# Five places for x, gate products with the narrow weight held in the array, and the samples' page attention with the pages as the moving operand

## The chip, the cores and the metric

The kernel runs on one core of one Trainium2 chip. The metric is the device time of one execution in microseconds, as a median over runs. The profiled execution is one more run of the same program; its trace is what the rows below are from.

## What is computed

One step of a decoder layer with two kinds of token: 528 prompt tokens (16 learned ones and 512 of the prompt) and 32 sample tokens (8 sequences of 4 new tokens, each with 256 cached tokens in two pages of 128). Cut to what matters here:

```python
xn = rmsnorm(h, norm_mix)                          # 560 rows of 2048
p  = xn @ w_in                                     # q, k, v, z, og of 8 + 8 heads, and three narrow parts:
a, b, f = p[..., C_A:C_Z] (2 x 8 columns), p[..., C_F:C_OG] (8 columns)
g, beta, logf = gates of a, b, f                   # per token and head
# attention of the samples, per head; c is the running sum of logf over page 0, page 1 and the new tokens
s = q @ k_past.T * scale + c_q - c_k               # 4 new tokens of a sequence against its own 256 cached ones
o = softmax([s, s_new]) @ [v_past, v_new]
```

Behind it come the gated delta rule of the other eight heads, the output product and a retrieval of experts for every token.

## The kernel before

One program runs its stages one behind the other, with a barrier of all engines between them: `norm_and_gates` (all 560 tokens, in tiles of 128, 128, 128, 128 and 48), then for the FIRST group of tokens (256: the 32 samples and 224 of the prompt) `heads`, `mix_out`, `ffn_norm` and `route`, then the same for the LATER group (304 tokens) with the gathering of experts beside it, then `rest_of_experts`. The traces name the tiles of the two `heads` stages `heads_a_...` and `heads_b_...`; the samples are in `heads_a` alone.

**norm_and_gates.** Rows of x come into two places (`lead.rows`), so tile i can be loaded when tile i - 2 has been turned. ScalarE squares and sums a tile (L432) and takes the root (L435), VectorE makes the reciprocal (L468) and scales the tile (L470), TensorE turns it in 16 blocks (L528), VectorE moves these out in four pieces, with the gain (L475), to `xnT`, the turned tokens. The 24 narrow columns (a, b, f) are made at the end: for each tile 16 products with `xnT` as the operand that is held in the array and the 24 columns of `w_narrow` streamed past it (L536). VectorE copies the result (L483) and the gates and running sums follow. Ahead of its first tile VectorE waits for the page table and makes row numbers of it (L458 to L463), from which GpSimd gathers cached values (L415).

**heads.** Each engine follows an order written down as marks in numbers: `Marks` runs several generators (the delta rule, the fox attention, the projections), each of which yields the mark of its next step, and the lowest mark goes first. TensorE's projections (L879, 16 products of 256 columns for each of 64 segments) lie between the other steps. `sampled` is TensorE's part for the samples' attention: it turns 16 pages of keys (L1051), makes the scores of the cached tokens with the pages held in the array and the 4 queries of a sequence as the moving operand (L1069, 16 products; L1063, L1066 and L1067 add the running sums), turns the scores (L1080), and after the exponential makes the output with 16 products that hold a page of values and move 4 columns (L1094). ScalarE and VectorE copy between these steps (L1586, L1592, L1593, L1326).

A product of 32-bit numbers stands in the trace as two instructions of TensorE (records, below), a transpose as one. In a row, `128*32` is partitions and columns of what is held in the array, and `128x128` what is streamed.

Of the kernel before, what the change touches and what calls it, by code (L numbers as in the profile page):

```python
# [22 lines left out]
ALU = mybir.AluOpType  # L23
# [6 lines left out]
P = 128  # L30
D = 2048
# [72 lines left out]
def constant_parts():  # L104
# [24 lines left out]
        "causal0": np.where(same0 & (col <= row) | (row >= NS), 0.0, NEG)[:, :NS],  # L129
        "batch_cols": np.broadcast_to((np.arange(NS)[None, :] // NQ == np.arange(NB)[:, None]).reshape(1, -1),  # L130
# [196 lines left out]
def norm_and_gates(nc, ins, outs, mem, scr, group):  # L327
# [4 lines left out]
        "const_in first_in vec_rows_in narrow_in bias_in pages_in x_in0 x_in1 x_squared x_root x_scaled x_turned "  # L332
# [6 lines left out]
            "cT": ([HEADS, 2, group.cols],),  # L339
# [3 lines left out]
        {"turn": [P, 4, 512], "nar": [P, T, 32], "cps": [HEADS, 2 * BANK], "vps": [P, P]},  # L343
# [12 lines left out]
    loaded = [16 * sum(len(parts[j]) for j in range(i % 2, i + 1, 2) if j >= early) for i in range(T)]  # L356
    with ctx:
        x, sq, ss, rt, rs = lead.rows, buf["sq"], buf["ss"], buf["rt"], buf["rs"]
# [7 lines left out]
        def _(sp):  # L366
            if samples:
                for rows, source in parts[0]:
                    sp.dma_start(x[rows, 0, :], source).then_inc(sem["x_in0"], 16)
# [51 lines left out]
        def _(act):  # L421
            if samples:
                act.wait_ge(sem["const_in"], 16)
            for i in range(T):
                r = group.rows[i]
                if i < early:
                    act.wait_ge(lead.landed[i], ready[i])
                else:
                    act.wait_ge(sem[f"x_in{i % 2}"], loaded[i])
                if i >= 1:  # L430
                    act.wait_ge(sem["x_squared"], i)
                nc.scalar.activation(sq[0:r, :], x[0:r, i % 2, :], ACT.Square, accum_out=ss[0:r, i:i + 1]  # L432
                                     ).then_inc(sem["x_squared"], 1)
# [2290 lines left out]
```

## Time and profile before

| | |
|---|---|
| median of 3 runs | 4275.11 us (4270.05 to 4278.51) |
| the profiled execution, its own time | 4273.7 us |
| its span, first to last instruction | 4271.9 us |
| granted TensorE clock, mean | 0.864 of 2.4 GHz |
| norm_and_gates | 0 to about 94 us |
| heads_a | about 94 to 936 us |

A row of the timeline gives the start from the span's start, the duration, the engine, the line and what it did, with xcount where several of one kind follow each other; behind it stands how long the engine was idle ahead and who ended that. A row of windows gives the busy time of each engine in a stretch with the number of instructions in brackets, then the granted clock (PEclk; 1.00 is 2.4 GHz, 0.50 is 1.2 GHz), the DMA engines' share and their rate.

### The profile page before, as it was taken

To read this page: it belongs to the slowest core of one execution; us is meant where nothing else is said; L and a number is where in the kernel's file an instruction comes from. 1 tells how busy PE (TensorE), PEld (TensorE's weight loads), DVE (VectorE), ACT (ScalarE), POOL (GpSimd) and SP (SyncE) were. 2 spreads that over 40 slices of the span, in tenths; PEclk is the share of its full clock that TensorE was granted. 3 is DMA by queue.
4 is the path that set the end of the run, shared out by engine and by line. 5 is a ranking of instruction groups with operands and counts; after the bars stand their busy time and mean duration, and the time that the engine had idled before them with its cause. 6 is when DMAs were issued, how large, how long until landed. Compare 5 with 4: busy or idle time off the path is not lost. (4 is left out here: it accounts for less than half of the span.)

```text
span 4271.9 us, 40765 instructions
## 1 busy us (share of the span) xinstructions
PE 3365.5 (79%) x14471; PEld 2616.6 (61%) x14471; DVE 2772.4 (65%) x4327; ACT 683.8 (16%) x1807; POOL 1587.5 (37%) x1091
## 2 busy tenths in 40 slices
PE   5999999989979999998949784000237999999994
PEld 5888888878856667666637563000136766666663
DVE  2233333320679999998986788699899655555655
ACT  1222222310112222223210011000124000000000
POOL 1000110100245555553563444588763322223222
PEclk7999999979989999999959897555555999999997
DMA  3766666648879999999999972899998999999997
GB/s 88 238 207 207 203 204 205 200 148 290 259 304 407 397 394 389 389 393 371 390 381 391 386 269 93 350 422 422 383 379 298 383 421 422 421 422 422 422 421 286
DMA packets 435530, 1396.72 MB, mean 327 GB/s; under 512 B 37188, under 2 KB 283608, under 8 KB 285264
## 3 DMA queue, kind: packets, MB, share of 16 engines
q0 software_dynamic: 125040, 890.66, 52.1%
q1 hardware_dynamic: 297616, 402.79, 27.3%
q10 hardware_dynamic: 12672, 100.67, 6.0%
q8 instruction: 115, 1.88, 0.2%
q14 instruction: 87, 0.71, 0.0%
HBM read 1258.98 MB, written 134.87 MB: 326 GB/s over the span
## 5 line engine op out<-in xcount | busy, mean ns | idle before, releaser
L1948 DVE CUSTOM_DVE_ANT_0 ex_ring<-ex_ring,ex_xi 128x2048 f32<-128x2048 f32 x544 | 1240.1, 2288 | 295.0 <-DMA ex_ring<-in_peer_u_dram,idx_all 205.3
L1899 POOL DMA_INDIRECT ex_ring<-in_peer_u_dram,idx_all x384 | 620.0, 1614 | 580.0 <-DVE ex_hid L1948 507.5
L1961 DVE SCALAR_TENSOR_TENSOR ex_y<-ex_ring,ex_wt,ex_y 128x2048 f32<-128x2048 f32 x285 | 677.9, 2379 | 233.3 <-DMA ex_ring<-in_peer_v_dram,idx_all 223.5
L879 PE MATMUL heads_b_pj<-xnT_later,lead 128*128 128x304 f32 x2048 | 595.6, 428 | 26.9 <-PEq L289 20.6
L1899 POOL DMA_INDIRECT ex_ring<-in_peer_v_dram,idx_all x256 | 397.4, 1552 | 571.9 <-DVE ex_y L1961 501.9
L2642 PE MATMUL rest_acc<-lead,rest_wide_act 128*128 128x512 f32 x1024 | 450.6, 598 | 6.6 <-DMA lead<-in_peer_v_dram 5.7
L879 PEld LDWEIGHTS heads_b_pj<-xnT_later,lead 128*128 128x128 f32 x2048 | 371.6, 194 | 134.5 <-issue 27.3
L2642 PE MATMUL rest_acc<-xnT_later,rest_wide_act 128*128 128x512 f32 x1024 | 444.7, 592 | 0.0
L2642 PEld LDWEIGHTS rest_acc<-lead,rest_wide_act 128*128 128x128 f32 x1024 | 304.2, 297 | 147.9 <-DMA lead<-in_peer_v_dram 7.1
L2642 PEld LDWEIGHTS rest_acc<-xnT_later,rest_wide_act 128*128 128x128 f32 x1024 | 302.1, 295 | 137.3
L1899 POOL DMA_INDIRECT ex_ring<-in_peer_u_dram,ex_idx_s x160 | 296.5, 1853 | 209.1 <-DVE ex_hid L1948 163.1
L2614 PE MATMUL rest_acc<-const,S_kept 128*128 128x128 f32 x4 | 1.4, 448 | 432.2 <-DVE S_kept L2667 432.2
L879 PE MATMUL heads_a_pj<-xnT_first,heads_a_w 128*128 128x256 f32 x1216 | 316.4, 398 | 2.4 <-DMA heads_a_w<-in_w_in_dram 2.4
L2614 PEld LDWEIGHTS rest_acc<-const,S_kept 128*128 128x128 f32 x4 | 0.6, 203 | 432.9 <-DVE S_kept L2667 432.9
L879 PEld LDWEIGHTS heads_a_pj<-xnT_first,heads_a_w 128*128 128x128 f32 x1216 | 226.7, 199 | 33.0 <-issue 2.9
L879 PE MATMUL heads_a_pj<-xnT_first,lead 128*128 128x256 f32 x832 | 213.7, 396 | 4.9 <-PEq L289 4.9
L1920 ACT ACTIVATE ex_act<-ex_hid 128x16 f32<-128x16 f32 x34 | 7.4, 216 | 1310.9 <-DVE ex_hid L1948 1310.9
L879 PEld LDWEIGHTS heads_a_pj<-xnT_first,lead 128*128 128x128 f32 x832 | 155.6, 199 | 25.6 <-issue 7.0
L2625 PE MATMUL rest_acc<-rest_hot_col,rest_hot_row 128*128 128x128 f32 x256 | 66.4, 441 | 103.4 <-DVE rest_hot_col L2692 103.4
L2054 PE MATMUL out_b_acc<-out_b_w,mixT_b 128*128 128x256 f32 (+1 forms) x672 | 147.4, 380 | 0.0
L2054 PEld LDWEIGHTS out_b_acc<-out_b_w,mixT_b 128*128 128x128 f32 (+1 forms) x672 | 111.5, 168 | 35.8 <-issue 4.7
L2625 PEld LDWEIGHTS rest_acc<-rest_hot_col,rest_hot_row 128*128 128x128 f32 x256 | 57.0, 328 | 112.9 <-DVE rest_hot_col L2692 112.9
(594 smaller groups left out, 4621.7 us busy)
## 6 DMA issues: line engine op xcount, KB each, us to landing
lead<-w_scratch SPq DMA_DIRECT2D x64, 1024.0 KB, 9.2
lead<-in_peer_v_dram SPq DMA_DIRECT2D x64, 1024.0 KB, 9.1
xnT_later<-in_peer_v_dram SPq DMA_DIRECT2D x64, 1024.0 KB, 9.0
heads_a_w<-in_w_in_dram SPq DMA_DIRECT2D x38, 1024.0 KB, 6.1
w_scratch<-heads_a_w ACTq DMA_DIRECT2D x38, 1024.0 KB, 4.6
lead<-in_w_in_dram SPq DMA_DIRECT2D x26, 1024.0 KB, 6.2
w_scratch<-lead ACTq DMA_DIRECT2D x26, 1024.0 KB, 4.4
out_a_w<-in_w_out_dram SPq DMA_DIRECT2D x7, 2048.0 KB, 14.0
```

What stands on the lines that cost most here:

```text
L879: last = nc.tensor.matmul(pj[j % PJ][:, 0:N], slot(j)[:, k, :], xnT[:, k, :], start=(k == 0), stop=(k == KT - 1))
L1899: pool.indirect_dma_start(self.ring[:, i % RING, :], None, self.tables[which], bass.IndirectOffsetOnAxis(ap=self.index(s, g, k), axis=0)). ...
L1920: self.nc.scalar.activation(self.act[:, g % 2, :], self.hid[:, g % 2, :], ACT.Gelu).then_inc(self.sem["activated"], 1)
L1948: nc.vector.tensor_tensor_reduce(ring, ring, self.tokens(s)[:], 1.0, 0.0, ALU.mult, ALU.add, self.hid[:, g % 2, k:k + 1]).then_inc(self.se ...
L1961: nc.vector.scalar_tensor_tensor(y, ring, wt, y, ALU.mult, ALU.add).then_inc(self.sem["consumed"], 1)
L2054: last = nc.tensor.matmul(acc[0:b - a, i, 0:GW], mixT[:, k, a:b], weights[:, k, :], start=(k == 0), stop=(k == KT - 1))
L2614: last = nc.tensor.transpose(acc[:, d, i * P:(i + 1) * P], source, cst("ident"))
L2625: last = nc.tensor.matmul(out, hot_row[:, n % 2, j, :], hot_col[:, n % 2, j, :], start=True, stop=True)
L2642: last = nc.tensor.matmul(acc[:, d, b:b + BANK], weights(d, quarter, c), v_place(n)[:, b:b + BANK], start=(n == 0), stop=(n == KEYS - 1))
```

## The change

It has two parts. In `norm_and_gates`: five places for x, so that SyncE issues all loads without waiting; ScalarE waits for the constants after its first square and no longer ahead of it; the row numbers of the pages are made after tile 1; the 24 narrow columns are made "flat", with `w_narrow` (24 columns) held in the array and 256 or 304 tokens streamed past it, those of FIRST after tile 3 and those of LATER at the end, then copied by ScalarE and turned back by five transposes. In `sampled`: queries and probabilities are spread over the eight sequences with zeros elsewhere (`q_apart`, `P_apart`), 32 columns each, and held in the array; the pages are streamed, 256 columns (both pages of a sequence) for the scores and 128 for the output. The results of four sequences lie in four groups of 32 output partitions, and two products with a constant (`strips`) add the four groups up.

```diff
@@ norm_and_gates, SyncE
-                if i >= 2:
-                    sp.wait_ge(sem["x_turned"], 4 * (i - 1))
-                for rows, source in parts[i] if i >= max(early, 1) else []:
-                    sp.dma_start(x[rows, i % 2, :], source).then_inc(sem[f"x_in{i % 2}"], 16)
+                for rows, source in parts[i] if i >= 1 else []:
+                    sp.dma_start(x[i][rows, :], source).then_inc(sem[f"x_in{i}"], 16)
...
-            for s in sorted(range(2), key=lambda s: T - 1 - (T - 1 - s) % 2):
-                sp.wait_ge(sem["x_turned"], 4 * (T - (T - 1 - s) % 2))
+            for s in range(2):
+                sp.wait_ge(sem["x_turned"], 4 * (s + 1))
@@ ScalarE
-            if samples:
-                act.wait_ge(sem["const_in"], 16)
...
+                if i == 0:
+                    act.wait_ge(sem["const_in"], 16)
                 act.wait_ge(sem["x_squared"], i + 1)
...
+            for n, (at, of) in enumerate(((0, FIRST), (BANK, LATER))):
+                act.wait_ge(sem["flat_done"], n + 1)
+                nc.scalar.copy(buf["flat"][:, of.base:of.base + of.cols], cps[:, at:at + of.cols]).then_inc(sem["flat_copied"], 1)
@@ VectorE
+                if i == 1:
+                    page_rows()
@@ TensorE
+                if i == 3 or i == T - 1:
+                    of, turned, at = (FIRST, mem["xnT"], 0) if i == 3 else (LATER, mem["xnT_later"], BANK)
+                    pe.wait_ge(sem["narrow_in"], 32)
+                    pe.wait_ge(sem["x_evac"], 4 * FIRST.n if i == 3 else 4 * T)
+                    for k in range(KT):
+                        last = nc.tensor.matmul(cps[:, at:at + of.cols], buf["w_narrow"][:, k, :], turned[:, k, :],
+                                                start=(k == 0), stop=(k == KT - 1))
+                    last.then_inc(sem["flat_done"], 1)
+            pe.wait_ge(sem["flat_copied"], 2)
             for i, (a, b) in enumerate(group.tiles):
-                for k in range(KT):
-                    last = nc.tensor.matmul(nar[0:b - a, i, 0:24], turned_place(k, i), buf["w_narrow"][:, k, :],
-                                            start=(k == 0), stop=(k == KT - 1))
+                last = nc.tensor.transpose(nar[0:b - a, i, 0:24], buf["flat"][:, a:b], cst("ident")[0:24, 0:24])
@@ heads, TensorE, sampled
-                for page in (1, 0):
-                    out = B.F1[:, page * NS:(page + 1) * NS].rearrange("p (b q) -> p b q", b=NB)
-                    nc.tensor.matmul(out, cst("after", P, 2 * P), past[:, :, page:page + 1].to_broadcast([P, NB, NQ]),
-                                     start=True, stop=False)
-                    if page == 0:
-                        nc.tensor.matmul(out, ones, later, start=False, stop=False)
-                    nc.tensor.matmul(B.F1[:, page * NS:(page + 1) * NS], ones, B.lU[:, 0:NS], start=False, stop=False)
-                    for b in range(NB):
-                        last = nc.tensor.matmul(B.F1[:, page * NS + NQ * b:page * NS + NQ * (b + 1)], B.kc[:, 2 * b + page, :],
-                                                q0[:, NQ * b:NQ * (b + 1)], start=False, stop=(b == NB - 1))
+                pe.wait_ge(sem["q_apart"], n)
+                for b in range(NB):
+                    strip = slice(b % 4 * NS, (b % 4 + 1) * NS)
+                    last = nc.tensor.matmul(B.F1[strip, 0:2 * P], B.q_apart[:, b, :],
+                                            B.kc[:, 2 * b:2 * b + 2, :].rearrange("p n c -> p (n c)"), start=(b < 4), stop=(b >= 4))
...
-                    last = nc.tensor.transpose(B.F2[0:NS, page * P:(page + 1) * P], B.sT[:, page * NS:(page + 1) * NS], ident)
+                    out, late = B.F2[0:NS, page * P:(page + 1) * P], B.lU[:, 0:NS] if page else B.late_q[:]
+                    nc.tensor.matmul(out, B.past_q[:, page, :], cst("after", P, 2 * P), start=True, stop=False)
+                    nc.tensor.matmul(out, late, ones, start=False, stop=False)
+                    last = nc.tensor.matmul(out, cst("strips"), B.sS[:, page * P:(page + 1) * P], start=False, stop=True)
...
-                nc.tensor.matmul(sums, B.f_vN[0:NS, 0, :], B.sPT[0:NS, 2 * NS:], start=True, stop=False)
-                for b in range(NB):
-                    for page in range(2):
-                        last = nc.tensor.matmul(sums[:, NQ * b:NQ * (b + 1)], B.vc[:, 2 * b + page, :],
-                                                B.sPT[:, page * NS + NQ * b:page * NS + NQ * (b + 1)],
-                                                start=False, stop=(b == NB - 1 and page == 1))
+                nc.tensor.matmul(sums[0:NS, :], B.sPT[:], B.f_vN[0:NS, 0, :], start=True, stop=False)
+                for i in range(4):
+                    for strip in range(4):
+                        b, page = 4 * (i // 2) + strip, i % 2
+                        last = nc.tensor.matmul(sums[strip * NS:(strip + 1) * NS, :], B.P_apart[:, b, page, :], B.vc[:, 2 * b + page, :],
+                                                start=(i == 0 and strip > 0), stop=(i == 3))
...
-                nc.tensor.transpose(B.F2[0:NS, 0:HD], B.sO[:], ident).then_inc(sem["s_rows"], 1)
+                nc.tensor.matmul(B.F2[0:NS, 0:HD], cst("strips"), B.sO[:], start=True, stop=True).then_inc(sem["s_rows"], 1)
@@ heads, VectorE
+                        order.mark(nc.vector.tensor_copy(B.past_q[:].rearrange("p n (b q) -> p n b q", b=NB), past))
+                        nc.vector.tensor_tensor(B.late_q[:], B.past_q[:, 1, :], B.lU[:, 0:NS], ALU.add
+                        nc.vector.tensor_tensor(B.q_apart[:], qkv[:, 0, 0:NS].unsqueeze(1).to_broadcast([P, NB, NS]),
...
-                        nc.vector.tensor_copy(B.sT[:], B.F1[:, 0:2 * NS]).then_inc(sem["scores_copied"], 1)
+                        nc.vector.tensor_copy(B.sS[:], B.F1[:, 0:2 * P]).then_inc(sem["scores_copied"], 1)
...
-                        order.mark(nc.vector.tensor_copy(B.sPT[:, 0:2 * NS], B.F1[:, 0:2 * NS]))
+                        order.mark(nc.vector.tensor_tensor(
+                            B.P_apart[:], B.F1[:, 0:2 * NS].rearrange("p (n q) -> p n q", n=2).unsqueeze(1).to_broadcast(shape),
```

The marks are as they were. TensorE's order in the second fox head, from before the scores to the turned scores, was this (the last number of a row is what comes out, L879 the projections, L970 the delta rule):

```order
L879 MATMUL heads_a_pj<-xnT_first,lead 128x256 x2
L1063 MATMUL heads_a_F<-heads_a_lpast,const 128x32
L1067 MATMUL heads_a_F<-heads_a_lU,const 128x32
L1069 MATMUL heads_a_F<-heads_a_f_qkvT,heads_a_kc 128x4 x8
L1063 MATMUL heads_a_F<-heads_a_lpast,const 128x32
L1066 MATMUL heads_a_F<-heads_a_lpast,const 128x32
L1067 MATMUL heads_a_F<-heads_a_lU,const 128x32
L1069 MATMUL heads_a_F<-heads_a_f_qkvT,heads_a_kc 128x4 x8
L1074 MATMUL heads_a_F<-heads_a_f_qkvT 32x32
L1075 MATMUL heads_a_F<-const,heads_a_lU 32x32
L1076 MATMUL heads_a_F<-const_first,const 32x32
L879 MATMUL heads_a_pj<-xnT_first,lead 128x256 x4
L970 MATMUL heads_a_R<-heads_a_yX,heads_a_EN 128x128 x2
L879 MATMUL heads_a_pj<-xnT_first,lead 128x256
L1080 MATMUL heads_a_F<-const,heads_a_sT 32x128 x2
```

The same place of the changed kernel (its L889 and L980 are the projections and the delta rule):

```order
L889 MATMUL heads_a_pj<-xnT_first,lead 128x256 x2
L1072 MATMUL heads_a_F<-heads_a_kc,heads_a_q_apart 32x256 x8
L1077 MATMUL heads_a_F<-heads_a_f_qkvT 32x32
L1078 MATMUL heads_a_F<-const,heads_a_lU 32x32
L1079 MATMUL heads_a_F<-const_first,const 32x32
L889 MATMUL heads_a_pj<-xnT_first,lead 128x256 x4
L980 MATMUL heads_a_R<-heads_a_yX,heads_a_EN 128x128 x2
L889 MATMUL heads_a_pj<-xnT_first,lead 128x256
L1084 MATMUL heads_a_F<-const,heads_a_past_q 32x128
L1085 MATMUL heads_a_F<-const,heads_a_late_q 32x128
L1086 MATMUL heads_a_F<-heads_a_sS,const_first 32x128
```

21 products stood ahead of L1074 and now 8; where two transposes stood, six products stand (the second three, for the other page, read `lU` in place of `late_q`). Nothing else moved on TensorE here; at the output 16 products of 4 columns became 16 of 128 columns in four groups of 32 partitions, in the same place.

On TensorE in `norm_and_gates` the changed kernel has this order, where all of tile 4's transposes used to come ahead of the 80 products of 24 columns:

```order
L532 MATMUL norm_a_turn<-const,norm_a_x_more 128x128 x32
L541 MATMUL norm_a_cps<-xnT_first,norm_a_w_narrow 24x256 x16
L532 MATMUL norm_a_turn<-const,norm_a_x_more 128x48 x16
L541 MATMUL norm_a_cps<-xnT_later,norm_a_w_narrow 24x304 x16
L546 MATMUL norm_a_nar<-const,norm_a_flat 128x24 x4
L546 MATMUL norm_a_nar<-const,norm_a_flat 48x24
```

32 products stand where 80 stood, and half of them ahead of the last tile's transposes.

## Rows read from the trace of the kernel before

**Rows 1.** The page: busy time and share of TensorE.
```profile
PE 3365.5 (79%) x14471; PEld 2616.6 (61%) x14471; DVE 2772.4 (65%) x4327; ACT 683.8 (16%) x1807; POOL 1587.5 (37%) x1091
```
**Rows 2.** Windows: heads_a with projections, and its last 49 us.
```profile
122.00:887.00 765.00, 748.07 (x4263) 652.01 (x4264) 253.05 (x746) 207.64 (x497) 76.13 (x86) 0.95 0.67 203
887.00:936.00 49.00, 38.77 (x188) 30.78 (x186) 11.92 (x31) 8.85 (x26) 2.85 (x2) 0.64 0.22 75
```
**Rows 3.** Timeline of norm_and_gates: start, us, engine, line, what, idle before.
```profile
10.83 1.91 ACT L432 ACTIVATE norm_a_sq<-lead 128x2048 f32<-128x2048 f32 x1 [1.65 <-DMA const<-in_constants_dram]
14.14 0.29 ACT L435 ACTIVATE norm_a_rt<-norm_a_ss,const 128x1 f32<-128x1 f32 x1
16.48 0.43 SPq L391 DMA_DIRECT2D pages<-in_page_table_dram  x1
20.28 0.17 DVE L458 CAST norm_a_rowf<-pages 128x16 f32<-128x16 int32 x1 [7.12 <-DMA pages<-in_page_table_dram]
20.84 0.16 DVE L468 RECIPROCAL norm_a_rs<-norm_a_rt 128x1 f32<-128x1 f32 x1
26.08 12.79 SPq L384 DMA_DIRECT2D lead<-in_x_prompt_dram  x3
26.70 0.15 DVE L468 RECIPROCAL norm_a_rs<-norm_a_rt 128x1 f32<-128x1 f32 x1
30.93 1.91 ACT L432 ACTIVATE norm_a_sq<-lead 128x2048 f32<-128x2048 f32 x1 [14.25 <-DMA lead<-in_x_prompt_dram]
79.72 0.53 DVE L483 COPY norm_a_narrow<-norm_a_nar 128x24 f32<-128x24 f32 x5 [30.35 <-PE norm_a_nar L536]
```
**Rows 4.** Timeline of TensorE in norm_and_gates: the last turned tile, the narrow products.
```profile
47.07 1.91 PE L528 MATMUL norm_a_turn<-const,lead 48*128 48x48 f32 x16 [2.95 <-DVE lead L470]
63.17 16.51 PE L536 MATMUL norm_a_nar<-norm_a_w_narrow,xnT_later 128*128 128x24 f32 x96
```
**Rows 5.** Windows of norm_and_gates: clock through the narrow products, and behind.
```profile
47.20:88.00 40.80, 35.41 (x193) 33.90 (x194) 3.65 (x18) 2.05 (x5) 0.00 (x0) 0.50 0.18 44
88.20:94.90 6.70, 1.83 (x16) 1.34 (x15) 2.04 (x11) 0.00 (x0) 0.00 (x0) 1.00 0.04 5
```
**Rows 6.** Timeline of the second fox head: a page copy, then the scores.
```profile
275.78 0.69 DVE L1582 COPY heads_a_kc<-heads_a_F 128x512 f32<-128x512 f32 x1 [1.41 <-PE heads_a_F L1051]
282.02 0.30 PE L1063 MATMUL heads_a_F<-heads_a_lpast,const 128*128 128x32 f32 x2
282.38 1.93 PE L1069 MATMUL heads_a_F<-heads_a_f_qkvT,heads_a_kc 128*128 128x4 f32 x16
284.17 0.39 PE L1063 MATMUL heads_a_F<-heads_a_lpast,const 128*128 128x32 f32 x2
287.21 0.32 PE L1074 MATMUL heads_a_F<-heads_a_f_qkvT 128*32 128x32 f32 x2
```
**Rows 7.** Timeline of TensorE: products with 32 held columns, and the output.
```profile
397.88 1.93 PE L994 MATMUL heads_a_R<-heads_a_state,heads_a_apart 128*32 128x128 f32 x16
399.75 1.99 PE L879 MATMUL heads_a_pj<-xnT_first,lead 128*128 128x256 f32 x8
402.23 4.00 PE L1094 MATMUL heads_a_F<-heads_a_sPT,heads_a_vc 128*128 128x4 f32 x32
```
**Rows 8.** Windows: through the scores, behind them, and behind the output.
```profile
282.70:286.00 3.30, 3.30 (x32) 3.30 (x31) 0.00 (x0) 0.00 (x0) 0.00 (x0) 1.00 0.97 236
286.10:292.80 6.70, 6.70 (x26) 5.69 (x27) 0.65 (x2) 0.00 (x0) 0.00 (x0) 0.50 0.12 33
405.60:408.90 3.30, 3.30 (x11) 2.76 (x11) 0.00 (x0) 0.19 (x1) 0.00 (x0) 0.50 0.47 114
```
**Rows 9.** Timeline of TensorE: 32 held columns, and two halves of the array's rows.
```profile
909.71 3.62 PE L1013 MATMUL heads_a_R<-heads_a_state,heads_a_apart 128*32 128x128 f32 x16
...
3241.80 11.16 PE L2631 MATMUL rest_acc<-rest_hot_col,rest_hot_row 64*128 64x128 f32 x64 [0.83 <-issue]
```
**Rows 10.** Window over the 64 records of the last row of rows 9.
```profile
3242.10:3253.00 10.90, 10.83 (x64) 10.27 (x62) 9.75 (x23) 6.08 (x25) 1.86 (x2) 0.50 0.84 283
```

More of the change, by code:

```diff
@@ L129, in constant_parts @@
         "causal0": np.where(same0 & (col <= row) | (row >= NS), 0.0, NEG)[:, :NS],
+        "strips": row % NS == np.arange(NS)[None, :],
         "batch_cols": np.broadcast_to((np.arange(NS)[None, :] // NQ == np.arange(NB)[:, None]).reshape(1, -1),
@@ L338, in norm_and_gates @@
             "bias": ([P, 3, HEADS],), "af": ([P, T, 16],), "ab": ([P, T, 16],), "ea": ([P, HEADS],),
-            "cT": ([HEADS, 2, group.cols],),
+            "cT": ([HEADS, 2, group.cols],), "x_more": ([P, T - 2, D],), "flat": ([24, group.cols],),
             **({"vec_rows": ([V_END, P],), "rowf": ([P, PAGES],), "rowi": ([P, PAGES], I32)}
@@ L355, in norm_and_gates @@
     ready = list(lead.counts)
-    loaded = [16 * sum(len(parts[j]) for j in range(i % 2, i + 1, 2) if j >= early) for i in range(T)]
+    assert early == 0
     with ctx:
-        x, sq, ss, rt, rs = lead.rows, buf["sq"], buf["ss"], buf["rt"], buf["rs"]
+        x = [lead.rows[:, i, :] if i < 2 else buf["x_more"][:, i - 2, :] for i in range(T)]
+        sq, ss, rt, rs = buf["sq"], buf["ss"], buf["rt"], buf["rs"]
         turn, nar, cps, vps = buf["turn"], buf["nar"], buf["cps"], buf["vps"]
@@ L368, in _ @@
                 for rows, source in parts[0]:
-                    sp.dma_start(x[rows, 0, :], source).then_inc(sem["x_in0"], 16)
+                    sp.dma_start(x[0][rows, :], source).then_inc(sem["x_in0"], 16)
                 lasting = mem["const"].shape[1]
@@ L421, in _ @@
         def _(act):
-            if samples:
-                act.wait_ge(sem["const_in"], 16)
             for i in range(T):
                 r = group.rows[i]
[L426 to L429, printed above, removed]
+                act.wait_ge(sem[f"x_in{i}"], 16 * len(parts[i]))
                 if i >= 1:
                     act.wait_ge(sem["x_squared"], i)
-                nc.scalar.activation(sq[0:r, :], x[0:r, i % 2, :], ACT.Square, accum_out=ss[0:r, i:i + 1]
+                nc.scalar.activation(sq[0:r, :], x[i][0:r, :], ACT.Square, accum_out=ss[0:r, i:i + 1]
                                      ).then_inc(sem["x_squared"], 1)
+                if i == 0:
+                    act.wait_ge(sem["const_in"], 16)
                 act.wait_ge(sem["x_squared"], i + 1)
@@ L455, in _, with page_rows @@
                                         0.5, None, ALU.mult).then_inc(sem["vecs_ready"], 1)
+            def page_rows():
                 dve.wait_ge(sem["pages_in"], 16)
@@ L541, in _ @@
             for i in range(T):
-                out, s = cps[:, i * P:(i + 1) * P], group.slot + i
+                out, s = cps[0:HEADS, i * P:(i + 1) * P], group.slot + i
                 block_of = min(s, 1)
@@ L648, in heads @@
                 "kc": ([P, PAGES, HD],), "vc": ([P, PAGES, HD],),
-                "sT": ([P, 2 * NS],), "sP": ([NS, KS],), "sPT": ([P, 3 * NS],),
-                "sO": ([P, NS],), "sN": ([NS, HD],), "smax": ([NS, 1],), "sden": ([NS, 1],), "srec": ([NS, 1],)}
+                "sS": ([P, 2 * P],), "sP": ([NS, KS],), "sPT": ([NS, NS],), "q_apart": ([P, NB, NS],),
+                "P_apart": ([P, NB, 2, NS],), "past_q": ([P, 2, NS],), "late_q": ([P, NS],),
+                "sO": ([P, HD],), "sN": ([NS, HD],), "smax": ([NS, 1],), "sden": ([NS, 1],), "srec": ([NS, 1],)}
                if samples else {"kT_kept": ([P, KA],), "v_kept": ([P, FIRST.n, HD],)}),
@@ L1325, in fox @@
                         act.wait_ge(sem["s_out"], n)
-                        nc.scalar.copy(B.sO[:], B.F1[:, 2 * P:2 * P + NS]).then_inc(sem["s_outT"], 1)
+                        nc.scalar.copy(B.sO[:], B.F1[:, 2 * P:2 * P + HD]).then_inc(sem["s_outT"], 1)
                     for i in range(1, T + 1):
```

31 lines of the change are left out of this document (17 added, 14 removed).

## The prediction

> **What bounds the kernel now.** The page comes first: TensorE is busy for 79% of the span [rows 1], and the stages run one behind the other, so what a stage loses or wins stays in the end time unless a later one gives it back. The next view is the windows by stage. From 122 to 887 us, heads_a with its projections, TensorE is busy for 748 of 765 us, VectorE for 253 and the DMA engines for 0.67 of it [rows 2]: TensorE is the bound there, and what is taken from it comes off the end. Its granted clock is 0.95 on the mean. The last 49 us of the stage have no projections left between the steps and a clock of 0.64 [rows 2].
>
> The timeline of norm_and_gates shows three things. VectorE stands idle for 7.1 us until the page table has landed, makes row numbers at 20.28 and starts tile 0 at 20.84, although ScalarE had its root at 14.43 [rows 3]. The third x tile is issued at 26.08, when its place is free, and ScalarE has it at 30.93 [rows 3]. From the end of the last turned tile, 48.98, to 79.72 nothing runs but 80 products of 24 columns [rows 3, 4], at 1.2 GHz [rows 5].
>
> **First stage, step by step.** ScalarE's first square loses its 1.65 us wait for the constants, so the root is there at 14.43 - 1.65 = 12.8 [rows 3]. VectorE has its gain vectors by then (they are what it did ahead of its 7.12 us of idling, 20.28 - 7.12 = 13.16). Tile 0 starts at 13.2 where it was 20.84: 7.6 us. A tile takes VectorE 26.70 - 20.84 = 5.86 us. The third x tile is issued behind the page table's row, 16.48 + 0.43 = 16.9, and needs 30.93 - 26.08 = 4.85 us [rows 3] and 2.4 of ScalarE (1.91, 0.29 and the reading of the sum): 24.2, where VectorE ends tile 1 at 13.2 + 2 x 5.86 = 24.9. So no load is waited for, and with 0.56 us for the row numbers (20.28 to 20.84) VectorE is through tile 3 at 37.2, TensorE's transposes 0.7 earlier.
>
> Then the flat products of FIRST: 16 of 256 columns. For their price I take a group of 32 held and 128 streamed columns, 16 records from 397.88 to 399.75, 0.117 us each, or 0.47 us for a product of 256 columns; at 1.2 GHz 16 such records took 3.62, 0.226 each, or 0.90 [rows 7, 9]. Sixteen cost 7.5 to 14.5 us; I take 9.5, since a stretch of streamed products with 8 held columns came ahead of the rise at 88.2 [rows 5]. Tile 4's transposes and last copy come to 2.4 (1.91 [rows 4] and half a us), and LATER's 16 products of 304 columns to 8.9 at 2.4 GHz (17.2 at 1.2). ScalarE's copy and five transposes I put at 1.5, an estimate from the 0.69 of a copy of 512 columns [rows 6] and 0.12 per record. Sum: 36.5 + 9.5 + 2.4 + 8.9 + 1.5 = 58.8 against 79.72: 21 us. All at 1.2 GHz gives 36.5 + 14.5 + 2.4 + 17.2 + 1.5 = 72.1, a gain of 8; all at 2.4 GHz, with shorter transposes, 54, a gain of 26. I take **-21**. The row numbers are made at 25 us instead of 20, and GpSimd's gather hides behind the flat products. Weights for heads_a are now loaded into places that come free after tiles 0 and 1, behind all x tiles in SyncE's queue.
>
> **Samples' attention, step by step, at 2.4 GHz.** Products that hold a page cost 16 records in 284.17 - 282.38 = 1.79 us, 0.112 each, whatever little they stream [rows 6]. Before, a head has 21 for the scores, 17 for the output and three transposes: 79 records, 8.8 us. After, if every product waits for the one ahead: scores 16 records of 256 columns, 32 x 0.112 = 3.6; the two sets of three products, 12 records with a change of shape in them at 0.117, 1.4; output 34 records, 3.8; the last product 0.3. That is 9.1, or **+0.3** a head, +3 us in all: as a plain rewrite it gives nothing. It pays if the four groups of 32 columns run at once. At best the scores cost 0.9 and the output 0.95 + 0.2, in all 3.8, **-5.0** a head.
>
> No row shows column groups side by side. The nearest is products on two halves of the array's rows: 64 records took 11.16 us at 1.2 GHz [rows 9, 10], 0.174 each with waits, where one group of columns took 0.226. The two halves do run beside each other, though in that order eight of one half stand ahead of eight of the other. The new order changes group after every product. I take most of the best, -4.3 a head, **-34** in all, and keep +3 and -40.
>
> A rule speaks against this. The Trainium skill, "TensorE: Matmul & The Clock Gate", Part 3, says that a load of weights overlaps products in flight only when they are on other rows of the array; the four groups share all rows. By it every load would be exposed. In the trace sixteen records on the same rows and the same columns took 0.117 each, with no room for an exposed load [rows 7]. The same part gives 2.4 times for three column groups, and by that figure the scores and output would cost about 2.7 us, an estimate between my two ends.
>
> **The clock.** While the scores run, TensorE is busy for all of the time with 4-column products at 2.4 GHz; right behind, 6.7 us are at 1.2 GHz, and after the output another 3.3 [rows 8]. In this time projections take twice as long. The windows put a size on it: (1 - 0.95) x 765 = 38 us lost at full rate in 765 us [rows 2]. Some 4 of it I leave to other places. After the change no long run of 4-column products is left; the group of 16 records with 32 held and 128 streamed columns has no fall behind it: 8 records of projections follow in 1.99 us, 0.25 each for 256 columns, the rate of 2.4 GHz [rows 7]. I take **-30**: all of the 34 but a little, and a few of the last 49 us. If the falls stay it is 0.
>
> **What is added elsewhere.** VectorE gets two small copies, `q_apart` (256 columns), a copy of 256 instead of 64 columns and `P_apart` (512 columns, 0.69 by the page copy [rows 6]): about 2 us a head, on an engine busy for a third of the time [rows 2]. Behind `q_apart` waits a delta-rule sum, behind `P_apart` the output; in both places TensorE has projections and delta-rule products ahead of the step that reads them. If both were exposed it would be 1.1 us a head, 9 in all. ScalarE's wider copy is hidden likewise. In the last head nothing covers them, 1 us. I add +1.
>
> **Sum.** 4273.7 (the profiled execution) - 21 - 34 - 30 + 1 = 4189.7. The median of the runs is 1.4 above that execution: **4191 us**.
>
> **Rivals.**
> - *The groups don't overlap.* For: no row shows it, and the rule above. Against: the halves of rows. 4191 + 37 = 4228.
> - *Overlap, but the clock still falls* as often: TensorE stands in shorter pieces then, and in the stage's last part, made of short pieces, it has 0.64 [rows 2]. 4191 + 30 = 4221. Neither: 4258.
> - *A new wait takes the place.* The output is short now, and behind it TensorE comes sooner to the sum that waits for VectorE's masked copy of u, begun with the output; scores come sooner after the page copies. If half of the 34 + 30 goes: 4223.
> - *The first stage gains little*, with x late or all at 1.2 GHz: 4204, within the first case's range.
> - *Slower.* One mechanism: the granted clock in heads_a stays at 1.2 GHz for long after each of the new groups. Every us at 1.2 costs half a us of streaming. With the other gains in place (85), it must be 170 us more, 21 us of each head's 102 (765 us hold seven and a half heads), before the kernel is slower. The old falls last 10 us a head, and the groups with 32 held columns caused none.
> - *No change* within 0.2% (8.6 us, what a measurement of this kernel can tell): the parts would have to cancel each other.
>
> **How the numbers follow.** Overlap and a steady clock 0.52, own range 4170 to 4212; no overlap 0.22; overlap with falls 0.08; a new wait 0.08; neither 0.05; no change 0.02; slower 0.03. The range reaches over the first four: 4170 to 4236. Faster 0.95, same 0.02, slower 0.03.
>
> **What would show it.** In the changed trace: VectorE's reciprocal of tile 0 at 13 us; the copy of the narrow results at 56 to 62 and heads_a's first projection near 74; PEclk of the windows through heads_a at 0.98 or more; eight products of the scores in about 1 us (overlap) or 3.5 (none), and heads 93 us apart instead of 102. It is wrong if the sampled products keep 0.2 us per 256-column record from start to start, if falls of the clock still follow them, or if TensorE shows idle time ahead of L1019's product or of the scores.

## The result and the profile after

The changed kernel takes 4166.9 us (median of 4 runs, 4166.22 to 4169.49) against 4276.81 of before (4 runs, 4270.05 to 4281.82): ratio 0.9748, 95% interval 0.9732 to 0.9763. The forecast was 4191 us, 4170 to 4236: the direction was right, and the time lies 3 us below the range. The same two kernels, measured once more among the experiments on the first stage, gave 4169.24 and 4271.89: a gain of 103 us where it is 110 here. The profiled execution took 4166.22 us, its span 4164.3, at a mean clock of 0.877.

The first stage, in the timeline of the changed kernel (ScalarE's third square, TensorE, and VectorE's copy of the narrow results; it answers to [rows 3, 4]):

```profile
23.73 1.91 ACT L427 ACTIVATE norm_a_sq<-norm_a_x_more 128x2048 f32<-128x2048 f32 x1 [6.95 <-DMA norm_a_x_more<-in_x_prompt_dram]
...
35.44 7.09 PE L541 MATMUL norm_a_cps<-xnT_first,norm_a_w_narrow 128*24 128x256 f32 x32
42.45 1.19 PE L532 MATMUL norm_a_turn<-const,norm_a_x_more 48*128 48x48 f32 x16
46.01 9.73 PE L541 MATMUL norm_a_cps<-xnT_later,norm_a_w_narrow 128*24 128x304 f32 x32 [2.36 <-issue]
...
56.72 0.53 DVE L487 COPY norm_a_narrow<-norm_a_nar 128x24 f32<-128x24 f32 x5 [10.86 <-PE norm_a_nar L546]
```

The narrow results are copied at 56.72 us where it was 79.72 [rows 3]. The flat products of FIRST took 7.09 us. Ahead of LATER's TensorE stands idle for 2.36 us, waiting for VectorE's four pieces of tile 4. The program asks for this wait, but VectorE stood idle for 0.50 and 1.08 us ahead of the last two pieces, which started at 44.06 and 45.50, while TensorE was through with the tile at 43.64; where none is late, in the trace of the first part alone, the idle time is 0.59 us. This comes up again in the last experiments.

The samples' attention in the third fox head (timeline of TensorE; it answers to [rows 6, 7]):

```profile
340.65 1.07 PE L1072 MATMUL heads_a_F<-heads_a_kc,heads_a_q_apart 128*32 128x256 f32 x16
341.54 0.22 PE L1077 MATMUL heads_a_F<-heads_a_f_qkvT 128*32 128x32 f32 x2
...
341.82 1.99 PE L889 MATMUL heads_a_pj<-xnT_first,heads_a_w 128*128 128x256 f32 x8
...
354.95 1.08 PE L1101 MATMUL heads_a_F<-heads_a_vc,heads_a_P_apart 128*32 128x128 f32 x32
355.96 0.92 PE L889 MATMUL heads_a_pj<-xnT_first,lead 128*128 128x256 f32 x3
```

The start of the next row tells what a group cost: 16 records of the scores, each of 256 columns, are through in 341.54 - 340.65 = 0.89 us, and the 32 of the output in 355.96 - 354.95 = 1.01. The projections right behind the scores run at 8 records in 1.83 us (341.82 to 343.65), which is the rate of 2.4 GHz, where [rows 8] had 1.2. The windows of before show the same from afar; here are those of the changed kernel:

```profile
103.60:816.70 713.10, 695.62 (x4287) 592.15 (x4285) 262.11 (x767) 209.60 (x502) 78.55 (x87) 1.00 0.71 220
816.80:834.70 17.90, 7.54 (x27) 4.49 (x27) 5.19 (x15) 7.32 (x20) 0.96 (x1) 0.69 0.10 30
```

For 713 us the clock does not fall once (0.95 in [rows 2]), and the fall to 1.2 GHz in the tail begins with 18 us left, not with 46. No wait of any size took the place of the old work (waits of TensorE in heads_a, changed kernel: us in total, times, longest):

```profile
PE heads_a_R L1045 <- DVE heads_a_gU L1550: 8.7, 8, 1.8
PE heads_a_R L953 <- DVE heads_a_qkvT L1472: 8.1, 8, 1.0
```

Before the change these two waits had the same 8.7 and 8.1 us. The only new one is 0.5 us, once, for ScalarE's exponential. From the first product of one stage to that of the next, in us:

| | before | changed | difference | forecast |
|---|---|---|---|---|
| norm_and_gates | 94.6 | 72.0 | -22.6 | -21 |
| heads_a | 841.9 | 762.8 | -79.1 | -63 |
| everything behind | 3335.4 | 3329.6 | -5.8 | 0 |

### The profile page after: what moved, and what is told of

It is laid out like the page before. It is cut to its first block and busy times, and to the rows that moved or that the text cites. A ratio compares the mean times of both kernels' runs of the same rounds, so it can differ in the third digit from the quotient of the medians.

```text
span 4164.3 us, 40395 instructions
## 1 busy us (share of the span) xinstructions
PE 3266.1 (78%) x14260; PEld 2508.1 (60%) x14260; DVE 2779.5 (67%) x4351; ACT 685.4 (16%) x1809; POOL 1607.5 (39%) x1091
## 5 line engine op out<-in xcount | busy, mean ns | idle before, releaser
L1916 POOL DMA_INDIRECT ex_ring<-in_peer_u_dram,idx_all x384 | 633.3, 1649 | 572.4 <-DVE ex_hid L1965 498.8
L889 PE MATMUL heads_b_pj<-xnT_later,lead 128*128 128x304 f32 x2048 | 594.2, 428 | 26.1 <-PEq L290 21.4
L889 PEld LDWEIGHTS heads_b_pj<-xnT_later,lead 128*128 128x128 f32 x2048 | 371.3, 194 | 133.9 <-issue 28.3
L889 PE MATMUL heads_a_pj<-xnT_first,heads_a_w 128*128 128x256 f32 x1216 | 302.5, 384 | 2.2 <-DMA heads_a_w<-in_w_in_dram 2.2
L889 PEld LDWEIGHTS heads_a_pj<-xnT_first,heads_a_w 128*128 128x128 f32 x1216 | 217.1, 191 | 31.3 <-issue 5.7
L889 PE MATMUL heads_a_pj<-xnT_first,lead 128*128 128x256 f32 x832 | 206.3, 385 | 4.9 <-PEq L290 4.9
L889 PEld LDWEIGHTS heads_a_pj<-xnT_first,lead 128*128 128x128 f32 x832 | 150.4, 192 | 24.8 <-issue 8.4
## 6 DMA issues: line engine op xcount, KB each, us to landing
out_a_w<-in_w_out_dram SPq DMA_DIRECT2D x7, 2048.0 KB, 14.7
```

The costliest lines, as they stand in the source:

```text
L889: last = nc.tensor.matmul(pj[j % PJ][:, 0:N], slot(j)[:, k, :], xnT[:, k, :], start=(k == 0), stop=(k == KT - 1))
L1916: pool.indirect_dma_start(self.ring[:, i % RING, :], None, self.tables[which], bass.IndirectOffsetOnAxis(ap=self.index(s, g, k), axis=0)). ...
```

## The experiments

**Each part alone.** One kernel with the edits inside `norm_and_gates`, one with all others; both are the diff shown above, cut in two.

> The kernel before with the first part alone (norm_and_gates). In the changed kernel heads_a begins 22.6 us earlier. Theory 1 (each part gives its gain in its own stage): 22 to 24 us less than before, 4252 to 4255, with the clock falls of heads_a as before. Rival (the earlier loads of the first weights or the earlier start shift something in heads_a, and this is where the surplus over the prediction comes from): 28 us or more less, with heads_a itself more than 4 us shorter than its 838.7.

> The kernel before with the second part alone (the samples' attention). Theory 1 (four column groups run wholly at once, 4.9 us a head at 2.4 GHz, and no fall of the clock is left, 4.2 us a head and some 12 us in the last 49 us of the stage): 80 to 88 us less than before, 4189 to 4197, PEclk 1.00 through heads_a. Rival (part of the surplus hangs on both parts together): under 76 us less.

Measured: first part alone 4238.61 us (4235.74 to 4243.11), 0.9917 of before (0.9901 to 0.9934), 34 less; second part alone 4193.74 (4190.93 to 4197.94), 0.9812 (0.9796 to 0.9829), 79 less. The second lies within the expected 4189 to 4197, though its gain is 1 us short of the expected 80 to 88. The first does not lie within its 4252 to 4255: of its 34 us its trace shows 22.3 in the stage itself, 3.3 in heads_a and 5.4 behind it, so the 28 or more of the rival came true in the sum but not by its reason: heads_a was not over 4 us shorter. The 3.3 are in the clock (table of heads_a below). The parts add up to 113 where both together gave 110, and 103 when measured again, within what the runs scatter.

**Column groups.** The changed kernel with all products of the scores and the output in the first 32 output partitions:

```diff
-                    last = nc.tensor.matmul(B.F1[strip, 0:2 * P], B.q_apart[:, b, :],
-                                            ..., start=(b < 4), stop=(b >= 4))
+                    last = nc.tensor.matmul(B.F1[0:NS, 0:2 * P], B.q_apart[:, b, :],
+                                            ..., start=(b == 0), stop=(b == NB - 1))
...
-                        last = nc.tensor.matmul(sums[strip * NS:(strip + 1) * NS, :], ...
+                        last = nc.tensor.matmul(sums[0:NS, :], ...
```

> The changed kernel with all sampled products in one group of 32 columns (output partitions 0 to 31; the other 96 rows of sS and sO are set to zero once), so that the same 24 products of a head follow each other. Theory 1 (overlap is worth 2.6 us at the scores and 2.6 at the output of each head, and the clock does not depend on it): 42 us over the changed kernel, 4207 to 4211, PEclk still 1.00. Rival (the dense use of four groups is what keeps the clock up): 70 us over it, 4237, with falls to 1.2 GHz behind the scores. Second rival (the page's rule: loads of weights on the same rows are exposed, 24 products more than streaming): over 0.115 us a record of 128 columns and 55 us or more over it.

Measured: 4202.57 us (4200.57 to 4208.13), 0.9833 (0.9817 to 0.985), 36 more than the changed kernel, heads 97.8 us apart where they were 92.6. Its windows and lines, the records of seven heads:

```profile
122.00:800.00 678.00, 664.06 (x3839) 561.44 (x3838) 236.65 (x697) 185.37 (x447) 67.92 (x76) 1.00 0.69 215
```
```profile
L1100 PE MATMUL heads_a_F<-heads_a_vc,heads_a_P_apart 128*32 128x128 f32 x224 | 25.8, 273 | 0.0
...
L1071 PE MATMUL heads_a_F<-heads_a_kc,heads_a_q_apart 128*32 128x256 f32 x112 | 25.5, 381 | 0.0
```

The same 16 records of the scores are busy for 25.5 / 7 = 3.64 us, where the rows of the changed kernel have 1.07, and the 32 of the output for 3.69 instead of 1.08. From the first start to that of the next work, as above, it is 3.48 instead of 0.89 and 3.61 instead of 1.01. So the groups overlap, and by almost all of the factor of four that is there: 3.9 and 3.6. The median is 4 us below the expected 4207 to 4211; heads_a is 42.9 us longer than in the changed kernel, where the expectation had 42. The clock stays at 2.4 GHz: it does not need the overlap.

**The clock alone.** The kernel before with its 4-column products unchanged in number and form, but put in pairs between the projections. Only marks differ:

```diff
                     for b in range(NB):
+                        if b % 2 == 0:
+                            yield at + 17 + 3.5 * (1 - page) + 0.85 * (b // 2)
...
+                    yield at + 31.5 + 0.7 * b
```

> The kernel before with its products of 4 columns unchanged in number and kind, but given out two at a time between projections (the marks of the sampled steps behind them are moved by 1 to 5). Theory 1 (what makes the clock fall is that 32 such products follow each other): the falls of heads_a with projections vanish, 4.2 us a head, 25 to 40 us less than before, 4236 to 4251. Rival A (the falls come with the number of such products, however they lie): within 8 us of before. Rival B (waits brought by the moved marks eat it): PEclk up to 0.99 but TensorE idle over 2 us a head.

Measured: 4240.3 us (4235.86 to 4244.58), 0.9924 (0.9907 to 0.994), 32 less than before with exactly the old work, and within the 4236 to 4251 of Theory 1. Its windows, and two rows of its timeline:

```profile
122.00:800.00 678.00, 662.72 (x3965) 580.13 (x3963) 228.02 (x667) 188.40 (x452) 68.53 (x76) 1.00 0.72 218
```
```profile
277.06 0.68 PE L879 MATMUL heads_a_pj<-xnT_first,lead 128*128 128x256 f32 x2
277.57 0.51 PE L1071 MATMUL heads_a_F<-heads_a_f_qkvT,heads_a_kc 128*128 128x4 f32 x4
```

The falls behind the scores and outputs are gone (1.00 for 0.95), and all that was gained is theirs: what made the clock fall was that 32 records of 4 columns followed each other without a pause, not their number. The last 49 us of the stage kept their low clock (33.8 us at 1.2 GHz for 36.0).

**Which run brings which fall.** The changed kernel with the scores new and the output in its old form (the lines of the output and its copies as in the removed half of the diff above):

> The changed kernel with the output of the samples' attention in its old form (pages of values held, 4 columns streamed, 32 records in one run), the scores in the new form. The output then costs about 3.8 us a head at 2.4 GHz where it is 1.3, 2.5 x 8 = 20 us more. Theory A, each long run of 4-column products brings its own fall of the clock: behind every output 3.4 us at 1.2 GHz, as before the change, another 1.7 us a head, 14 in all: 4201 (4197 to 4205), heads about 96.8 us apart, and the windows through heads_a at about 0.97. Theory B, the fall behind the output needed the one behind the scores just ahead of it: no falls, 4187 (4183 to 4191), heads 95.1 us apart, clock 1.00.

Measured: 4206.0 us (4202.89 to 4209.15), 0.984 (0.9825 to 0.9855). Theory A holds, 1 us above its range. The output of the third fox head and the windows behind it:

```profile
367.04 4.45 PE L1100 MATMUL heads_a_F<-heads_a_sPT,heads_a_vc 128*128 128x4 f32 x32
371.34 4.61 PE L889 MATMUL heads_a_pj<-xnT_first,lead 128*128 128x256 f32 x10
```
```profile
165.00:765.00 600.00, 587.17 (x3402) 503.88 (x3401) 207.62 (x612) 163.95 (x400) 61.15 (x67) 0.97 0.68 210
...
371.30:374.80 3.50, 3.50 (x9) 2.87 (x10) 0.00 (x0) 0.18 (x1) 0.00 (x0) 0.50 0.09 26
```

One run of 32 4-column records is enough: in every head with projections the clock is at 1.2 GHz behind it, for 3.4 and 6.8 us in turn (heads 96.4 and 98.1 us apart); in this head it had fallen 1.4 us before the run's end, at 369.9. The sum came out as expected, its parts did not: by the table below 14.7 us are the instructions, where the expectation had 20, and 25.1 the clock, where it had 14.

**All of heads_a in one account.** If TensorE's work goes at half rate at 1.2 GHz, then each us there costs half a us, and the stage's length less that half should depend on the instructions alone. The middle columns are sums over the pieces of the granted clock in each trace:

| | heads_a | of it at 1.2 GHz | half of that | the rest |
|---|---|---|---|---|
| before | 841.9 | 111.1 | 55.6 | 786.3 |
| first part alone | 838.6 | 101.3 | 50.7 | 787.9 |
| before, products spread | 806.8 | 42.2 | 21.1 | 785.7 |
| new form, one column group | 805.7 | 24.1 | 12.1 | 793.6 |
| new scores, old output | 802.6 | 68.7 | 34.4 | 768.2 |
| second part alone | 765.7 | 24.9 | 12.5 | 753.2 |
| changed | 762.8 | 18.6 | 9.3 | 753.5 |

Kernels with the same instructions in this stage have the same rest within 2.2 us, whatever their clock, and the seven further kernels below with the stage of the changed one lie at 752.7 to 753.9. So the account can be trusted: of the 79.1 us, 46.3 came from the clock and 32.8 from the instructions; the scores bring 18.1 of these and the output 14.7. With one column group the new form costs 7.3 us more than the old. Of the 46.3 us of the clock, 32.4 lie behind scores and outputs (64.9 us at 1.2 GHz, against none), 12.4 in the tail of the stage (36.0 us, against 11.1) and 1.4 in its start, ahead of the first scores (10.2 us, against 7.5).

**The first stage taken apart.** The changed kernel with the 80 old narrow products behind the last tile (and the five places kept), and with the old flow of x (and the flat products kept). Of the second, this is the wait that comes back; the wait for the constants ahead of the first square and the row numbers ahead of tile 0 come back as well:

```diff
+                if i >= 2:
+                    sp.wait_ge(sem["x_turned"], 4 * (i - 1))
```

> The changed kernel with the narrow products in their old form (80 products of 24 streamed columns behind the last tile), the five places for x and all else kept. If the flat form is worth the larger part of the first stage, the products take about 31 us from 43.6 us on (48.98 to 79.72 before), the narrow results are copied at 74.4 instead of 56.7 us: 17.7 us more, 4185 (4181 to 4189). Rival, the early start of the tiles is what gained and the clock of the changed first stage is higher anyway, so that the old products run at 2.4 GHz for half of their time: 7 to 10 us more, 4174 to 4177.

> The changed kernel with the old flow of x: two places, ScalarE's first square behind the constants, the row numbers of the pages ahead of tile 0; the flat narrow products and the samples' attention stay new. Before the change the last tile was turned at 48.98 us, with the five places at 43.64. If the parts simply add up, the flat products are worth 17.7 (measured with the old narrow products) and the flow of x the other 5 to 6: first product of heads_a at 77.5 us and 4173 (4169 to 4177). Rival: the flow of x was hidden behind the flat products of FIRST, which hold TensorE until 42.5 anyway, and undoing it costs 2 us or less: 4167 to 4170. Other rival: with the slower flow the granted clock is 1.2 GHz through both flat products, and the stage ends 12 us or more later: 4179 to 4183.

> The changed kernel itself once more, for a direct comparison on the same chip: 4167 (4163 to 4171), and the first product of heads_a at 72 us. What lies behind heads_a, from the first product of the output stage to the end, took 3335.4 us before, and 3329.6 (changed) and 3330.0 (first part alone) with the new first stage. If that difference of 5 to 6 us is real it shows here again (3328 to 3331); if it is the spread of executions, any value from 3328 to 3337 can come.

Measured: old narrow products 4186.79 us (4180.85 to 4189.49), 0.9791 (0.9776 to 0.9806); two places 4171.94 (4169.76 to 4173.58), 0.9757 (0.9742 to 0.9772); the changed kernel again, on the chip of the first of these, 4169.24 (4163.35 to 4175.56), 0.9756 (0.9742 to 0.9769). The flat products carry the stage: without them heads_a starts at 88.3 us. The flow of x is worth 3 to 5 us in the medians, and 0.4 to 4 by the ratios, since the kernel before, measured beside each, was at 4274.5, 4271.9 and 4276.8: near or below what can be told. Its start of heads_a is at 78.7. The repeated kernel's profile has that start at 77.8, not 72.0, with the same code: its flat products took 7.81 and 11.19 us, in part at 1.2 GHz, and VectorE's last pieces of tile 4 came late. So a single profile places the first stage to some 6 us. Behind heads_a it had 3325.2 us. All fourteen profiles, in which that part of the program never changed, lie between 3325.2 and 3336.4, so the -5.8 of the first comparison is within the spread of single profiles. Whether a part of it is an effect stays open: the three kernels with the whole old first stage lie at 3333.7 to 3335.8, the mean of the eleven others is 3329.3.

**Column groups in the first stage as well.** If four groups run at once, the flat products can use them:

```diff
+                        strip = slice(k % 4 * 32, (k % 4 + 1) * 32)
-                        last = nc.tensor.matmul(cps[:, at:at + of.cols], buf["w_narrow"][:, k, :], turned[:, k, :],
-                                                start=(k == 0), stop=(k == KT - 1))
+                        last = nc.tensor.matmul(cps[strip, at:at + of.cols], buf["w_narrow"][:, k, :], turned[:, k, :],
+                                                start=(k < 4), stop=(k >= KT - 4))
...
-                last = nc.tensor.transpose(nar[0:b - a, i, 0:24], buf["flat"][:, a:b], cst("ident")[0:24, 0:24])
+                last = nc.tensor.matmul(nar[0:b - a, i, 0:24], buf["flat"][:, a:b], cst("strips")[:, 0:24], start=True, stop=True)
```

> The changed kernel with the flat narrow products of the first stage also spread over the four groups of 32 output partitions: w_narrow is padded with zeros to 32 columns, product k writes group k mod 4, and the product with the constant `strips` that turns the flat result back adds the four groups up. If four groups run at once here as they did in the samples' scores, the 16 products of FIRST take about 1.8 us instead of 7.1 and those of LATER 2.4 instead of 9.7; in front of LATER's stands VectorE's last tile, so FIRST's saving is worth what TensorE was late for tile 4, 42.45 less 38.1, some 4 us. Sum 4 + 7.3: 11 us less than the changed kernel, 4156 (4151 to 4161). Rival: the clock, which was 2.4 GHz through the flat products, falls when they are short, and what follows at 1.2 GHz takes the gain back: 4163 to 4168.

Measured: 4159.84 us (4157.76 to 4163.38), 0.9734 (0.972 to 0.9747), the changed kernel beside it 4169.24: 9 us less, and within the expected 4151 to 4161, though the two intervals overlap a little. The timeline of TensorE and ScalarE:

```profile
40.85 2.25 PE L544 MATMUL norm_a_cps<-xnT_later,norm_a_w_narrow 128*32 128x304 f32 x32 [1.00 <-issue]
49.56 2.19 PE L549 MATMUL norm_a_nar<-const_first,norm_a_flat 128*128 128x24 f32 x10 [6.46 <-ACT norm_a_flat L437]
```
```profile
49.09 0.41 ACT L437 COPY norm_a_flat<-norm_a_cps 128x304 f32<-128x304 f32 x1 [9.88 <-remote]
```

The 32 records take 2.25 us instead of 9.73, and then 6 of the 7.5 us won are stood idle: ScalarE's copy comes at 49.09, though the products that it waits for ended at 43.10. Three more kernels asked why: VectorE makes the copy; GpSimd's gathers are left out (zeros in place of the cached gate values); the gathers start after tile 4.

> The kernel with the flat products in four groups, and LATER's flat result copied by VectorE instead of ScalarE. In that kernel's trace TensorE ends LATER's flat products at 43.1 us and ScalarE copies them at 49.09 only, six us later, 1.6 us behind the end of GpSimd's last gather (47.48) and without anything that the program makes it wait for. Theory: the delay belongs to ScalarE (its next instructions are not there), VectorE copies at 43.3 and the stage ends 5 to 6 us sooner: first product of heads_a at 61, 4154 (4150 to 4158). Rival: the delay belongs to what is copied, TensorE's results being there or being told of only once GpSimd's gathers are through: VectorE copies at 49 as well, 4160 (4156 to 4164).

> The kernel with the flat products in four groups, without GpSimd's 16 gathers of the cached gate values: they are replaced by zeros, so this part of the samples' input is left out. In all profiles of the new first stage something waits between 42 and 49 us without cause in the program: VectorE for its last pieces of tile 4 (changed kernel, 1.08 and 0.50 us; the same again, 1.8 and 0.8), or ScalarE for its copy (6.0 us in the kernel with four groups). GpSimd's gathers run from 25 to 47 us. Theory A, the gathers hold these handoffs up: without them the copy follows LATER's flat products (43.1 us) at once, heads_a starts at 60 to 61 us, 4154 (4150 to 4158). Theory B, the waits have another source: a wait of 2 to 6 us stays between 42 and 49, heads_a starts at 65 us or later, 4160 (4156 to 4164).

> The kernel with the flat products in four groups, with the row numbers of the pages made after tile 4 instead of tile 1, so that GpSimd's gathers run from about 41 to 63 us. Theory A, the gathers hold handoffs up: the waits move with them, into the chain of copies and gates between 43 and 62 us, and since GpSimd's drain comes at 65, heads_a starts at 66 to 70 us, 4160 to 4164. Theory B, the waits between 42 and 49 us have another source (a fixed time of the stage): they stay where they are, and the stage ends as with the gathers at 25 us, at 66 to 67, 4160. Both give a similar time; what tells them apart is the place of the waits in the timeline. If instead the gathers delay handoffs only in their last third, from 42 to 49 us, then with late gathers the copy follows at 43 us and the waits appear at 57 to 65.

Measured: 4160.93 us (4154.53 to 4162.63) with VectorE's copy, 4154.54 (4154.41 to 4162.72) without the gathers, 4158.94 (4157.06 to 4161.54) with late ones. The times differ by little, and each trace is one execution (for the kernel without the gathers the slowest of its four). With VectorE's copy neither theory held as written: the copy came at once (LATER's products ended at 50.3, the copy stands at 50.36), but now VectorE's pieces of tile 4 had been late, 1.08 us and more, and the products started at 46.02. So the delay belongs neither to ScalarE alone nor to that result. ScalarE's copy without the gathers, and then with late ones:

```profile
43.87 0.41 ACT L434 COPY norm_a_flat<-norm_a_cps 128x304 f32<-128x304 f32 x1 [3.53 <-PE norm_a_cps L541]
```
```profile
43.94 0.41 ACT L437 COPY norm_a_flat<-norm_a_cps 128x304 f32<-128x304 f32 x1 [3.53 <-PE norm_a_cps L544]
```

In both the wait is gone. Without the gathers heads_a starts at 61.4 us, 5 earlier. With late ones it starts at 66.0, since the stage now ends with GpSimd: its last gather is issued at 61.36, and TensorE's first projection waits 9.2 us for the barrier where it otherwise waits 4.9.

The gathers are the suspect, but that they cause the delays is not shown. In five profiles in which they run from 25 us on, a result of TensorE that fell due between 42 and 49 us was taken up 0.4 to 6 us late. In two others, the first part alone and the one column group, with the same first stage and the last gather issued at 46.7 and 46.9, nothing was late. This is VectorE in the latter, the four pieces of tile 4 without a pause:

```profile
45.69 1.15 DVE L477 TENSOR_TENSOR xnT_later<-norm_a_turn,vecs 128x192 f32<-128x192 f32 x4 [6.19 <-PE norm_a_turn L532]
```

So the expectation's "in all profiles of the new first stage something waits" was wrong, gathers alone are not enough, and two profiles without a delay are few. That the late gathers held up nothing at their start tells little, and at their end no handoff was due. A gather that starts ahead of tile 0 and ends by 42 us, and several profiles of each kernel, would tell more; neither was tried.

## Why the prediction was right and where it was wrong

- **What bounds heads_a: right.** TensorE had no new wait but one of 0.5 us, and all that was taken from it came off the end.
- **The groups overlap: right,** and nearly in full. I took -4.3 a head of a possible -5.0. With the clock taken out the account gives 32.8 / 8 = 4.1. At one group the form costs 7.3 us more than before, where I had +3. The Trainium skill, "TensorE: Matmul & The Clock Gate", Part 3, would have every load exposed when the row group is the same, and then 0.89 us for 16 records could not be: the trace contradicts it, 3.9 times faster than one group (3.48 / 0.89). The same part's 2.4 times for three groups agrees in kind. The 2.7 us that I worked out from it do not follow: 3.6 us for the scores and 3.6 for 32 records of the output, over 2.4, make 3.0.
- **The clock: the step that failed.** Its mechanism was right: no falls are left behind scores and outputs. Its size was -30 and is -46.3. Behind the scores and outputs it was put at 34 and then at "all but a little" of it; it measured 32.4. The tail of 49 us, 36.0 of it at 1.2 GHz, was counted with "a few": it fell to 11.1 us at 1.2 GHz, worth 12.4. The last 1.4 lie in the start of the stage, and nothing here shows why. The row for the tail stood in [rows 2], a clock of 0.64 over 49 us: 18 us lost at full rate. The old form of the samples' products was part of what kept it there: 33.8 us of the tail are at 1.2 GHz with the old products spread, 23.3 with new scores and the old output, 16.0 with the new form in one group. A sum of 34 and "a few" is also not 30; I rounded down a term that I had the numbers for.
- **The first stage: near in size,** -22.6 for -21 in the first profile and -16.8 in the second of the same code, with steps that were wrong and in part cancel. Tile 0 came at 13.25 for 13.2, held by the gain vectors; the root was there at 11.69, not 12.8. "No load is waited for" was wrong: the third x tile was issued at 16.75 and ScalarE had it at 23.73, 7.0 us later where I had 4.85, and VectorE stood idle for 1.49. Transposes at 2.4 GHz made up for it. FIRST's products took 7.09 us instead of 9.5. LATER's took 9.73 instead of 8.9, 2.8 us of them at 1.2 GHz (8.35 in the first part alone, all at 2.4), and tile 4's pieces came late.
- **What is added elsewhere: right as far as seen.** The two waits for VectorE kept their 8.7 and 8.1 us; the +1 can't be told apart.
- **What the miss is made of.** The profiled execution fell by 107.5, the forecast by 84: 23.5 more. 16.3 are the clock, 5.8 lie behind heads_a, within the spread of single profiles, and 1.6 in the first stage; the instructions of heads_a gave 0.2 less. With the clock alone at its size the forecast would have been 4191 - 16 = 4175, inside the range: that the time fell out of it took the spread as well.
- **The range** ended 21 us below the forecast. The prediction does not say how 4170 is made: its best cases of 26, 40 and 34 give 4176. The largest unknown, the clock, had no bound of its own downwards.

## What to carry to other kernels

Where small products stream few columns, hold the small operand (32 columns, zeros for what isn't wanted), stream the big one, and change the group of 32 output partitions after every product: four run in the time of one. Ask of each such stretch what clock it leaves behind; the clock gave more here (46 us, 32 of them behind runs of 4-column products) than the products themselves were made shorter (33), and two fifths of the second part's gain were to be had by spreading the old products alone (32 of 79 us). When a clock's cost is a term, add it up over all windows of the stage, its tail too, and take the range from there.

## What the runs showed of the hardware

- Four groups of 32 output partitions on the same rows ran at once: 16 records of 256 columns in 0.89 us from the first start to the next work, 3.48 in one group; 32 records of 304 columns busy for 2.25 us, 8.35 in one group, both at 2.4 GHz.
- The granted clock fell to 1.2 GHz behind or near the end of 32 records of 4 columns, with TensorE busy for all of the time, and did not fall when the same records stood 4 at a time between projections, nor behind 32 records of 128 columns in one group (heads 97.8 us apart, 1.00 throughout).
- While GpSimd's 16 gathers ran, in five profiles a result of TensorE that fell due between 42 and 49 us was taken up 0.4 to 6 us late by ScalarE or VectorE; in two others with the same gathers none was, and in one without them and one with them started at 42 us none was either. The cause is not shown.
